# The index stage by halves, its keys out of the first products, and seven products ahead of row 0

## The reference, cut to what matters

```python
h = x @ w_in                                   # 1024 -> 648 columns
c_q, k, v, k_idx, w_idx = split(h, [256, 384, 512, 640])
c_q = rms_norm(c_q, g_cq)
q = (c_q @ w_uq).reshape(T, 16, 64)
q_idx = (c_q @ w_iq).reshape(T, 8, 128)
k_idx = layer_norm(k_idx, g_ik, b_ik)
q, k = apply_rope(q), apply_rope(k)            # first 16 of 64 columns
q_idx, k_idx = apply_rope(q_idx), apply_rope(k_idx)   # first 32 of 128 columns
score = einsum('qh,hqs->qs', w_idx, relu(einsum('qhd,sd->hqs', q_idx, k_idx)))
sel = top_k(where(causal, score, -inf), 64)
# softmax attention of 16 heads over the selected keys, then @ w_o, layer norm, a gated MLP, ...
```

## Time and profile before

| | us |
|---|---|
| median of 3 runs | 996.75 (994.36 to 997.92) |
| the profiled execution | 988.9 |
| its span, first to last instruction | 987.2 |
| PE busy | 944.6 (96%) |
| DVE busy | 606.8 (61%) |
| ACT busy | 464.2 (47%) |
| POOL busy | 138.3 (14%) |
| granted TensorE clock, mean | 0.998 |

### The profile page before, as it was taken

One profiled execution on the slowest core, in us unless ns is written; L12 is line 12 of the kernel. 1 busy time (PEld: TensorE's weight loads), 2 busy tenths in 40 slices (PEclk: granted clock), 3 DMA queues, 4 the chain that ended last, 5 costly groups with the idle time before them and its releaser, 6 DMA issues.

```text
span 987.2 us, 11869 instructions
## 1 busy us (share of the span) xinstructions
PE 944.6 (96%) x4717; PEld 779.5 (79%) x4717; DVE 606.8 (61%) x960; ACT 464.2 (47%) x616; POOL 138.3 (14%) x115
## 2 busy tenths in 40 slices
PE   6779999999999998999999999999999999999996
PEld 5657788888887787998788888877787778888885
DVE  4674676464648756978755464585323567767775
ACT  4565344252433453254443433345566465556562
POOL 3163200000001810001100000001174110101010
PEclk9999999999999999999999999999999999999999
DMA  8891356556547653224765655467433355555531
GB/s 281 189 165 34 120 191 199 184 185 199 173 154 228 231 175 108 88 83 128 247 200 173 199 182 187 154 212 256 152 132 123 128 169 190 175 180 187 186 129 42
DMA packets 103510, 165.89 MB, mean 168 GB/s; under 512 B 3931, under 2 KB 72570, under 8 KB 103456
## 3 DMA queue, kind: packets, MB, share of 16 engines
q1 hardware_dynamic: 99968, 152.61, 47.0%
q0 software_dynamic: 3488, 12.53, 5.7%
HBM read 160.93 MB, written 4.19 MB: 167 GB/s over the span
## 4 chain that ended last, share of the span: by engine, by line
PE 84%; DVE 9%; ACT 3%; DMA 2%; issue 1%; POOL 1%; DVEq 0%; POOLq 0%; ACTq 0%
PE PG L1758 12%; PE PG L1760 12%; PE PG L1759 12%; PE PA L1758 12%; PE PA L1760 11%; PE PA L1759 11%; PE PA L2161 2%; DVE wlo L586 1%; PE PG L1890 1%; ACT whi L577 1%; PE TB L2292 1%; PE TB L1907 1%; PE TB L2002 1%; DVE xlo L1070 1%; DVE stats L1132 1%
## 5 line engine op out<-in xcount | busy, mean ns | idle before, releaser
L586 DVE TENSOR_TENSOR wlo<-raw,whi 128x2048 fp32r<-128x2048 f32 (+1 forms) x129 | 300.5, 2345 | 80.5 <-ACT whi L577 80.4
L577 ACT ACTIVATE whi<-raw 128x2048 fp32r<-128x2048 f32 (+1 forms) x142 | 268.5, 1907 | 52.6 <-PE PA L1760 19.5
L1758 PE MATMUL PG<-whi,xlo 128*128 128x512 f32 x560 | 223.2, 399 | 4.0 <-DVE wlo L1288 2.9
L1760 PE MATMUL PG<-whi,xhi 128*128 128x512 f32 x560 | 219.1, 391 | 0.0
L1759 PE MATMUL PG<-wlo,xhi 128*128 128x512 f32 x560 | 218.7, 391 | 0.0
L1758 PE MATMUL PA<-whi,xlo 128*128 128x512 f32 (+1 forms) x344 | 137.5, 400 | 10.1 <-DVE xlo L1070 5.2
L1760 PE MATMUL PA<-whi,xhi 128*128 128x512 f32 (+1 forms) x344 | 132.7, 386 | 0.0
L1759 PE MATMUL PA<-wlo,xhi 128*128 128x512 f32 (+1 forms) x344 | 132.4, 385 | 0.0
L1758 PEld LDWEIGHTS PG<-whi,xlo 128*128 128x128 f32 x560 | 105.8, 189 | 26.0 <-DVE wlo L1288 3.3
L1760 PEld LDWEIGHTS PG<-whi,xhi 128*128 128x128 f32 x560 | 105.5, 188 | 22.6
L1759 PEld LDWEIGHTS PG<-wlo,xhi 128*128 128x128 f32 x560 | 105.8, 189 | 20.6
(11 more groups left out here) (264 smaller groups left out, 1084.2 us busy)
## 6 DMA issues: line engine op xcount, KB each, us to landing
raw<-in_ffn_w_gate SPq DMA_DIRECT2D x44, 512.0 KB, 4.0
raw<-in_ffn_w_up SPq DMA_DIRECT2D x44, 512.0 KB, 5.0
raw<-in_ffn_w_down SPq DMA_DIRECT2D x22, 1024.0 KB, 4.8
raw<-in_w_up SPq DMA_DIRECT2D x44, 512.0 KB, 4.8
raw<-in_hgrn_w_in SPq DMA_DIRECT2D x16, 1024.0 KB, 5.3
raw<-in_w_qkv SPq DMA_DIRECT2D x12, 1024.0 KB, 5.2
raw<-in_w_down SPq DMA_DIRECT2D x11, 1024.0 KB, 4.9
raw<-in_att_w_o SPq DMA_DIRECT2D x4, 1024.0 KB, 5.7
```

The source lines that it names most:

```text
L577: nc.scalar.activation(whi[:, g, 0:n_], raw[:, s, 0:n_], ACT.Copy).then_inc(S("w_hi"), 1)
L586: nc.vector.tensor_tensor(wlo[:, s, 0:n_], raw[:, s, 0:n_], whi[:, g, 0:n_].bitcast(F32), ALU.subtract).then_inc(S("w_lo"), 1)
L1758: mm(dst, xl[:, k, rows], whi[:, g, cols], start=first, stop=False)
L1760: return mm(dst, xh[:, k, rows], whi[:, g, cols], start=False, stop=last_)
```

## The change

- The two first units hold columns 0 to 256 (c_q) and 392 to 648 (most of v, index keys, head weights); the later unit 2 holds columns 256 to 392 (k and v's first eight). Each of the four pieces is loaded in two DMAs with runs of 256 columns. `pin` is laid out anew, and its last eight columns of c_q are overwritten by v's once `cqn` is made.
- One power on POOL serves c_q's and the index keys' variance.
- Seven products with dropped results (HEAT) run on PE between turning row 0 and row 0's first products; row 1 is turned ahead of tile 6 in the first stage only.
- On PE, `cqn` is turned after six of unit 2's eight tiles; w_iq's products run in two halves of the heads, the turned index keys between them; q's turns and scores alternate by two heads; w_uq's first half goes to `PG`; five and four more warming products are run, and k is turned after w_uq's.
- On DVE, `lo(2)` and `lo(3)` come earlier, index keys are done ahead of `xlo` of `cqn`, and `qi` is roped in two halves. The rope and the copies of k are on POOL, behind the last head's sum.
- On ACT, `hi(3)` comes earlier, `hi(6)` moves from ahead of the relus to behind them, and the table load of Exp comes ahead of q's first copy.

```diff
-WARM = 5
+WARM, HEAT = 5, 7
...
-C_K, C_V, C_KI, C_WI = 256, 384, 512, 640
+SKIP, EARLY = 392, 256
+C_V, C_KI, C_WI, C_K = 248, 376, 504, 512
...
-    a = up(w_in, 0)
-    a.append([(0, 8, IN_COLS - 512, w_in.rearrange("(t p) n -> p t n", p=P)[:, :, 512:IN_COLS])])
+    v = w_in.rearrange("(t p) n -> p t n", p=P)
+    a = [[v[:, 4 * j:4 * j + 4, c:c + EARLY] for c in (0, SKIP)] for j in range(2)]
+    a.append([(0, 8, SKIP - EARLY, v[:, :, EARLY:SKIP])])
...
+                    dst = raw[:, u, g * UNIT // 2:(g + 1) * UNIT // 2].rearrange("p (t s c) -> p t s c", s=2, c=EARLY)
+                    for s, view in enumerate(units[u]):
+                        sp.dma_start(dst[:, :, s, :], view[:, 2 * g:2 * g + 2, :]).then_inc(S(landed_), 16)
...
-            power(C_CQ)
-            power(C_KEY)
+            power(C_IN)
...
+            pool.wait_ge(S("k_in"), 2)
+            pool.wait_ge(S("iacc"), 2 * HI)
+            link(rope(pool, link, pin[:, :, C_K:C_K + P].rearrange("p r (g c) -> p r g c", g=2), 2, ROT, 0))
+            for r in range(RT):
+                for c in range(2):
+                    ins = pool.tensor_copy(kd[:, r, :, c, :],
+                                           pin[:, r, C_K:C_K + P].rearrange("p (g c) -> p g c", g=2))
...
+            act.wait_ge(S("cqn"), 1)
+            full(2)
+            ac.activation(pin[:, :, C_K:C_K + P], PA[:, 2:4, 0:P], ACT.Copy).then_inc(S("k_in"), 1)
+            ac.activation(pin[:, :, C_V:EARLY], PA[:, 2:4, P:SKIP - EARLY], ACT.Copy).then_inc(S("k_in"), 1)
...
+            act.wait_ge(S("iq_first"), 1)
+            ac.activation(qi[:, :, 0:HALF], PA[:, 0:2, :], ACT.Copy).then_inc(S("qi_a"), 1)
             e = ev["ki"]
             turned(e)
-            ac.activation(flat(kT), TB[:, e % 2, :], ACT.Copy).then_inc(bank_free(e), 1)
-            turned(e + 1)
-            ac.activation(kiT, TB[:, (e + 1) % 2, 0:T], ACT.Copy).then_inc(bank_free(e + 1), 1)
-            copy_turned("qi", qiT)
-            hi(6)
+            ac.activation(kiT, TB[:, e % 2, 0:T], ACT.Copy).then_inc(bank_free(e), 1)
+            full(U_IQ)
+            ac.activation(qi[:, 1, HALF:D], PA[:, 3, :], ACT.Copy).then_inc(S("qi_a"), 1)
+            def index_turned(g):
+                e = ev["qi"] + g
+                turned(e)
+                ac.activation(flat(qiT[:, 2 * g:2 * g + 2, :]), TB[:, e % 2, :], ACT.Copy).then_inc(bank_free(e), 1)
+            index_turned(0)
+            index_turned(1)
             for hd in range(HI):
 
                 act.wait_ge(S("iscore"), hd + 1)
                 if hd >= 2:
                     act.wait_ge(S("iacc"), 2 * (hd - 1))
                 ac.activation(relu[:, hd % 2, :], PA[:, hd % 4, 0:384], ACT.Relu).then_inc(S("relu"), 1)
-            for f in range(2):
+                if hd in (1, 3):
+                    index_turned(2 + hd // 2)
+            hi(6)
+            act.wait_ge(S("ssq"), RT)
+            ac.activation(sq[:, 0, 0:1], sq[:, 0, 0:1], ACT.Exp, scale=0.0)
...
+            lo(3)
+            vec.wait_ge(S("pin"), 1)
+            for r in range(RT):
+                ins = ve_.bn_stats(stats[:, r, 0, :], pin[:, r, C_KI:C_WI])
+            link(ins)
+            for r in range(RT):
+                ins = ve_.bn_aggr(mv[:, 2 + r, :], stats[:, r, 0, :])
+            link(ins)
+            ve_.tensor_scalar(ve[:, 2:4], mv[:, 2:4, 1], LN_EPS, None, ALU.add)
             vec.wait_ge(S("ssq"), RT)
...
-            lo(3)
-            full(2)
-            link(ve_.tensor_copy(pin[:, :, 512:IN_COLS], PA[:, 0:2, 0:IN_COLS - 512]))
...
+            lo_of_bank(flat(xlo[:, 0:2, :]), ev["cq"], flat(xhi[:, 0:2, :]))
+            vec.wait_ge(S("trig"), 1)
+            rope(ve_, link, pin[:, :, C_KI:C_WI].rearrange("p r (g c) -> p r g c", g=1), 1, ROTI, ROT)\
+                .then_inc(S("ki_r"), 1)
+            vec.wait_ge(S("reldist"), 1)
+            ve_.tensor_scalar(relv[0:HQ, 0:T], PG[0:HQ, 0, 0:T], -1.0, None, ALU.mult).then_inc(S("relv"), 1)
+            ve_.memset(relv[0:HQ, T:REL_W], -NEG).then_inc(S("relv"), 1)
             lo(4)
+            vec.wait_ge(S("ki_r"), 1)
+            for f in range(2):
+                if f:
+                    full(U_IQ)
+                    ve_.tensor_copy(qi[:, 0, HALF:D], PA[:, 2, :]).then_inc(S("qi_b"), 1)
+                    vec.wait_ge(S("qi_b"), 1)
+                    vec.wait_ge(S("qi_r"), 1)
+                vec.wait_ge(S("qi_a"), f + 1)
+                q_half = qi[:, :, f * HALF:(f + 1) * HALF].rearrange("p r (g c) -> p r g c", g=HI // 2)
+                rope(ve_, link, q_half, HI // 2, ROTI, ROT).then_inc(S("qi_r"), 1)
...
+                if u == 0:
+                    pe.wait_ge(S("x_hi"), 1)
+                    for _ in range(HEAT):
+                        mm(PA[:, 0, :], xhi[:, 0, 0:P], xhi[:, 0:4, 0:P], start=True, stop=True)
...
-                            if r == 0 and k == 7:
+                            if r == 0 and k == (7 if u else 6):
...
+            def later_columns(ks):
+                for k in ks:
+                    for r in range(RT):
+                        last = products(PA[:, 2 + r, 0:136], k, r, U_IN + 2, slice(k * 136, (k + 1) * 136), k == 0,
+                                        k == KT - 1)
+                return last
...
+            later_columns(range(6))
             e = ev["cq"]
             pe.wait_ge(S("cqn"), 1)
...
+            later_columns(range(6, KT)).then_inc(S("w_used"), 1)
+            parts_ready(ev["c0"])
+            pe.wait_ge(S("pin"), 1)
+            mm(PG[0:HQ, 0, 0:T], relT[0:BUCKETS, :], hot[0:BUCKETS, :], start=True, stop=True).then_inc(S("reldist"), 1)
+            def halves(u, f, bank):
+                for r in range(RT):
+                    for t in range(2):
+                        last = products(bank(r), t, r, u, slice(t * D + f * HALF, t * D + (f + 1) * HALF),
+                                        t == 0, t == 1)
+                return last
+            lower, upper = lambda r: PA[:, r, :], lambda r: PA[:, 2 + r, :]
             parts_ready(e)
+            pe.wait_ge(S("w_lo"), U_IQ + 1)
+            halves(U_IQ, 0, lower).then_inc(S("iq_first"), 1)
+            e = ev["ki"]
+            pe.wait_ge(S("ki_r"), 1)
+            t_bank(e)
+            for r in range(RT):
+                last = nc.tensor.transpose(TB[:, e % 2, r * P:(r + 1) * P], pin[:, r, C_KI:C_WI], ident[:, :])
+            last.then_inc(S("t_full"), 1)
+            pe.wait_ge(S("k_in"), 2)
+            halves(U_IQ, 1, upper).then_inc(S("w_used"), 1)
+            def scores(g):
+                parts_ready(ev["qi"] + g)
+                for hd in (2 * g, 2 * g + 1):
+                    if hd >= 4:
+                        pe.wait_ge(S("relu"), hd - 3)
+                    mm(PA[:, hd % 4, 0:128], qiT[:, hd, 0:P], kiT[:, 0:P], start=True, stop=True)
+                    mm(PA[:, hd % 4, 128:384], qiT[:, hd, P:T], kiT, start=True, stop=True).then_inc(S("iscore"), 1)
+            pe.wait_ge(S("qi_r"), 1)
+            turn_rows("qi", qi, events=range(2))
+            parts_ready(ev["ki"])
+            scores(0)
+            for g in range(1, 4):
+                if g < 3:
+                    pe.wait_ge(S("qi_r"), 2)
+                    turn_rows("qi", qi, events=(g + 1,))
+                scores(g)
             pe.wait_ge(S("relv"), 1)
-            down(U_IQ, 0, True, True)
-            e = ev["ki"]
+            pe.wait_ge(S("w_lo"), U_UQ + 1)
+            halves(U_UQ, 0, lambda r: PG[:, r, :]).then_inc(S("first_q"), 1)
+            pe.wait_ge(S("relu"), HI)
+            halves(U_UQ, 1, lower).then_inc(S("w_used"), 1)
+            def keep_warm(n_):
+                for _ in range(n_):
+                    mm(PA[:, 3, :], xhi[:, 4, 0:P], flat(xhi[:, 4:6, :]), start=True, stop=True)
+            keep_warm(WARM)
...
+                keep_warm(4)
```

More of the change, by code:

```diff
@@ L559, in build @@
         for u in range(U_ALL + RING):
-            two = any(u - up_unit(U, i) in (0, 1) for U in (U_F0, U_F1, U_F2) for i in range(NFF))
+            two = u < 2 or any(u - up_unit(U, i) in (0, 1) for U in (U_F0, U_F1, U_F2) for i in range(NFF))
             total[u % RING] += 32 if two else 16
@@ L752, in _ @@
             hi(2)
+            hi(3)
             act.wait_ge(S("ang"), 1)
@@ L1290, in _ @@
             x_lo_rows("x", 1)
+            lo(2)
             vec.wait_ge(S("pos"), 48)
@@ L2031, in _ @@
             last.then_inc(S("t_full"), 1)
-            pe.wait_ge(S("w_lo"), 3)
-            for k in range(KT):
-                for r in range(RT):
-                    last = products(PA[:, r, 0:136], k, r, U_IN + 2, slice(k * 136, (k + 1) * 136), k == 0, k == KT - 1)
-            last.then_inc(S("w_used"), 1)
-            parts_ready(e)
-            mm(PA[0:HQ, 2, 0:T], relT[0:BUCKETS, :], hot[0:BUCKETS, :], start=True, stop=True).then_inc(S("reldist"), 1)
+            def later_columns(ks):
[4 more added lines that the diff above has]
+                return last
```

(3 more changed lines are left out.)

84 lines of the change are left out of this document (16 added, 68 removed).

## The result

The kernel after took 985.54 us (median of 4 runs, 980.71 to 987.94), the kernel before 995.78 beside it: 0.989 of the time, 95% interval 0.984 to 0.994, a gain of 10.2 us. Forecast were 988.0 and a range of 985.0 to 994.0. The time lies in the range, but 2.5 us from the forecast, and the steps that led there did not all hold. The profiled execution took 987.94 (span 986.0), just 1.0 less than the profiled one of before, where the sum had 8.8. So the first question of the experiments is where these 7.8 us are, the second why the median moved more than the sum.

A forecast was written before the change was run, and what follows sets the result against it. The chain to attention was taken as the bound, DVE alone holding its end (47.17 to 63.99 us). Terms -2.0 - 1.7 - 6.0 + 0.45 + 0.45 = -8.8 us took the median 996.75 to 988.0, range 985.0 to 994.0.

The forecast's parts named there:

- a gain on the path carries over: From the profiled execution (988.9 us) to the median (996.75, 7.85 above): the path's -8.8 us was applied unchanged to the median.
- Products run ahead, row 1 sooner: Start: seven dropped products raise PE's clock earlier (1.2 us), row 1 is turned a tile sooner; together -2.0 us.
- Eight loads: First loads: eight DMAs with 1 KB runs instead of four cost 0, up to 0.5 us, since a full queue hides later issues.
- Rival (b): Start: the first loads come late and the front gains nothing, 990 to 991 us; chance 0.08.
- Key chain and order of unit 2: Ahead of the index products: key chain off the path, `cqn` turned after six of eight tiles; -1.7 us.
- Halves: Index stage: w_iq's products and rope in two halves bring the first head 8.7 us after the first index product; -6.0 us.
- Head loop: Index scores on DVE: turns of tiles 4 to 7 between heads on PE and ACT cost 0.45 us.
- Entry to attention: Before pair 1's logits: PE's last turns and warming products, behind k and q on POOL, cost 0.45 us.
- Rival (a): Entry to attention: POOL's rope and copies of k and q become the path, 990.7 to 993.7 us; chance 0.15.
- (c): Attention, pair 1: the `rel_scratch` store delays the last output weights, a stall of 2 to 3 us, 990 to 991; chance 0.05.
- Rival (d): Ahead of attention: PE's clock drops to 1.2 GHz through four pairs, adding 17.7 us, 1011 us; chance 0.05.
- theory A: Set after the measurement: path gain about 8.8 us less the loads' cost; the rest is PE's clock falling behind 1-3 us idles.

The follow-up runs named there:

- e3: The kernel before with only the seven dropped products and the earlier turn of row 1: 995.42 us, ratio 0.9992 to before.
- e1: The kernel before with each of its four first loads split by columns into two (256 KB, runs of 1 KB): 996.36 us, ratio 1.0006.
- e2: The kernel before with each of its four first loads split by input tiles into two (256 KB, runs of 2 KB): 996.88 us, ratio 1.0013.
- e8: The kernel before with eight first loads split by columns, the second block read from column 392 instead of 256: 996.67 us, ratio 1.0007.
- e10: The kernel after with four of its eight first loads issued on ACT's queue instead of SP's: 982.39 us, ratio 0.9871 to before.
- e9: The kernel after, but ACT's first copy of the index queries waits for all of w_iq's products instead of half: 990.70 us, ratio 0.9945 to before.
- e12: The kernel after with four first loads on ACT's queue, eleven more dropped products in attention and nine in the turn at 365 us: 980.32 us, ratio 0.9855.
- e6: The kernel after with five more dropped products ahead of the output turn in pair 3 of attention: 982.63 us, ratio 0.9872 to before.
- e4: The kernel after without its seven dropped products at the start: 986.47 us, ratio 0.9905 to before.
- e7: The kernel after with twelve dropped products at the start in place of seven: 984.12 us, ratio 0.9895 to before.
- e5: The kernel before with 11 dropped products ahead of turning the index queries and 10 ahead of the query products: 989.77 us, ratio 0.9946.

## Why the prediction was right or wrong

The sum of the path held to about 0.4 us. The step that failed is its last one, that "a gain on the path carries over" unchanged from an execution of 988.9 us to a median of 996.75; it stands on a second one, that TensorE's clock, once risen, stays. What the runs showed in their place: some 6.7 us of before's usual time are falls of the clock that its profile lacks, and how many of them remain is not the same before and after.

- **Products run ahead, row 1 sooner (-2.0).** Right with four loads and a load that lands in time (e3: to the digit). What failed is the step that the clock rises 4 us after work begins and then stays: PE idled 1.84 us behind the seven products, and the clock fell again at 12. Worth some 1.5 us here (the estimate above). The rise itself came sooner than the 4.0 us of the sum: in e3 the products are 0.23 us apart from 9.83 on, 3.5 us after the dropped ones began at 6.31, and DVE's pieces held the rest.
- **Eight loads (0, up to 0.5).** Failed in size: 0.5 to 0.8 in e1, e2 and e8, 1.84 in the profiled execution. The runs of 1 KB, put at 0, cost 0.15 us for each 512 KB (1.5 against 1.35 in e2); that a full queue hides the rest does not hold to the end, since e10 gets 0.5 back by issuing from two queues. Rival (b) came in with this part. The estimate between two figures of the Trainium skill (DMA: Bandwidth & Descriptors, section Bandwidth) had 3.5 us for pieces of this size; the runs say 1.5 us for each 512 KB, some 350 GB/s: its warning had the right sign, and two to five times the size.
- **Key chain and order of unit 2 (-1.7).** Right: 6.84 us against 6.85.
- **Halves (-6.0).** Right: 8.80 against 8.7, and e9 takes back 2.80 of it for the products' share.
- **Head loop (+0.45).** Wrong: 0. The heads' sums stayed 0.85 apart, so ACT's and PE's turns fit beside them.
- **Entry to attention (+0.45), POOL.** The copies of k took 0.25 us each and not 0.45; k's part 2.5 us and not 3.3. The cost was right all the same, 0.51: ahead of its turns PE still waits for POOL's rope (0.86 us) and for ACT's copy (0.83). In e12, without a fall, the logits stand 0.34 from the mark. Rival (a) did not occur, nor (c), though the store was issued only 2.7 us earlier (32.79 against 35.47) and not 5.3.
- **Rival (d), the clock.** Its mechanism was right and its form wrong. It was set as one fall that lasts through four pairs for 17.7 us, to be feared only if POOL were slow. What the runs show are short falls behind idle times of 0.5 to 2.9 us, some 3 to 10 us long and 1.0 to 3.5 us dear, several in an execution, in both kernels. The argument against it (before idled 2.92 us and stayed fast) came from one execution, and e1 and e2, the same kernel but for its first loads, fell just there, as did e3. The Trainium skill (TensorE: Matmul & The Clock Gate, Part 1) has idleness throttle the engine; the runs agree in kind, with idle times shorter than those that it warns of (0.85 and 0.83 us in e6).
- **"A gain on the path carries over" from 988.9 to the median.** This is the step that missed the median. By the runs with a mean clock of 0.998, before takes 989.1 (988.9 to 989.3, four runs) and after 980.71 (one run): 8.4 us on the path, against 8.8. Before's median is 6.7 above its value, after's 4.8. So 8.4 + 1.9 is the measured 10.2, but for rounding; with four runs after and an interval of 5 us either way, the 1.9 by itself is within the noise. It fits what the traces show: the change removes PE's idle times of 2.92 and 2.36 us, behind which e1, e2 and e8 have one or two falls of 1.0 to 1.5 us each, and which the profile after and those of e4, e6 and e7 do not have. The 7.85 us between profile and median in the sum were falls, and were taken as a constant.
- **The profiled execution.** Forecast -8.8, found -1.0. The difference of 7.8: start +2.9, head loop, entry and rounding -0.3, fall at 76 us +3.2, 0.3 between there and 362 us, fall at 374 us +1.5, and 0.2 around the span.
- **Small slips in the sum.** The chances of the forecast and (a) to (c) add up to 0.88, not 0.87. For the low end, "no loss on entry" takes 0.45 off 987.95, which gives 987.5 and not 987.1. Neither changes the forecast.

Open: e3's whole fits theory A, but why one execution falls behind a given idle time and the next does not, no run shows. That the start of the best run after has no fall is inferred from e6 (copy at 22.59; -6.2 and the 2.2 us less give -8.4), since that run has no trace.

## What to carry over

Compare the profiled execution with the median before anything else: a gap of 0.8% with a mean clock of 0.998 in the profile says that most runs have something that this trace lacks, and a change that fills or opens idle times of TensorE moves that gap as well as the path. A step that saves a microsecond and leaves TensorE idle for one or two may give it all back (e3); dropped products in such gaps near the critical path showed no cost (e5's best runs took 988.6 us, before's 988.9), and brought the usual time near the best one (e5, e12). Whether a single fall is cured can't be read from one profile, since the same gap falls in some executions and not in others: compare the mean clocks of many runs. Work that is meant to bridge a wait has to be sized for a late end of that wait; seven products were too few for the latest first load seen, and no run shows how many are enough.

## What the runs showed of the chip

- Idle times as short as 1.09 and 0.53 us, one behind the other, were followed by 7 us at a granted clock of 0.5 in six profiles; the same two in five others (before, e3, e4, e5, e10) were not.
- A fall costs 1.0 to 3.5 us of the time by its place: 1.0 to 1.5 in the index stage, 3.2 to 3.5 in pair 3 of attention, 1.5 to 1.8 at 374 to 384 us, 1.1 at 677. The mean granted clock of a run tells how many there are: in the profiles 0.997 or more goes with none, 0.996 with one, 0.994 with two (e10), 0.991 to 0.993 with three, 0.989 with four (e1, e7, e8, e9), 0.987 with five (e2); e3 has 0.989 with three, one of them 10 us long. Before took 989 us at 0.998, 991 to 992 at 0.994, 993 to 995 at 0.991, 995 to 997 at 0.989, 997 to 999 at 0.987.
- Loads of 256 KB, eight in a queue, came at 1.5 us for 512 KB with runs of 1 KB (e1, e8, after) and at 1.35 with runs of 2 KB (e2), against 1.25 to 1.34 for four of 512 KB with runs of 2 KB.
- On POOL a 128x32 product of a rope takes 0.24 us and a 128x128 copy 0.25, where a 128x128 sum or product takes 0.46 and a cast to bytes 1.1.
